# A decoder trunk with a mixture of experts on one Trainium2 core: the experts' down weights loaded as row pairs, the activation transposed by even and odd columns

## The reference

```python
D_MODEL = 1024; SEQ = 256; N_EXPERTS = 8; TOP_K = 2; D_FF_EXPERT = 3584
# moe_w_gate, moe_w_up: (1, 8, 1024, 3584)      moe_w_down: (1, 8, 3584, 1024)

def moe_swiglu(h, w_router, w_gate, w_up, w_down):
    t = h.reshape(-1, D)
    logits = (t @ w_router).astype(jnp.float32)
    top_v, top_i = lax.top_k(logits, TOP_K)
    top_w = jax.nn.softmax(top_v, axis=-1)
    combine = jnp.sum(jax.nn.one_hot(top_i, N_EXPERTS, dtype=jnp.float32) * top_w[..., None], axis=1)
    out = jnp.zeros_like(t)
    for e in range(N_EXPERTS):
        y = (jax.nn.silu(t @ w_gate[e]) * (t @ w_up[e])) @ w_down[e]
        out = out + combine[:, e:e + 1].astype(t.dtype) * y
    return out.reshape(B, S, D)
```

## Time and profile before

| | us |
|---|---|
| median of three runs | 1368.86 |
| the three runs | 1368.86, 1367.09, 1369.31 |
| the profiled execution, its own time | 1367.2 |
| its span (first to last instruction) | 1365.5 |
| PE busy | 1343.2 |
| DVE busy | 1086.4 |
| ACT busy | 924.5 |
| POOL busy | 127.3 |

### The profile page before, as it was taken

How to read it: one execution, slowest core, us unless ns; L and a number is a source line. 1 busy time by engine, 2 the same in 40 slices (tenths; PEclk the granted TensorE clock), 3 DMA queues, 4 the chain that set the end, 5 groups by cost and what they waited for, 6 DMA issues and landing times.

```text
span 1365.5 us, 17334 instructions
## 1 busy us (share of the span) xinstructions
PE 1343.2 (98%) x7271; PEld 1132.4 (83%) x7272; DVE 1086.4 (80%) x714; ACT 924.5 (68%) x755; POOL 127.3 (9%) x145
## 2 busy tenths in 40 slices
PE   8999999999999999999999999999999999999997
PEld 7878999989678888888888888888888888888885
DVE  5756444466768888888888888888888888888996
ACT  6664333355667777777777777777777777777774
POOL 3310000012124700000000000010000000000010
PEclk9999999999999999999999999999999999999999
DMA  9745555646439999999999999999999999999993
GB/s 317 230 148 183 185 185 185 201 129 214 143 124 285 395 391 369 397 389 377 388 391 364 371 395 383 368 397 389 369 376 396 374 377 383 394 370 376 397 396 145
DMA packets 200501, 431.78 MB, mean 316 GB/s; under 512 B 9697, under 2 KB 45793, under 8 KB 200418
## 3 DMA queue, kind: packets, MB, share of 16 engines
q1 hardware_dynamic: 195568, 416.19, 84.4%
q0 software_dynamic: 4848, 14.42, 2.9%
q10 hardware_dynamic: 2, 0.00, 0.0%
HBM read 418.58 MB, written 7.35 MB: 312 GB/s over the span
## 4 chain that ended last, share of the span: by engine, by line
PE 97%; DVE 1%; ACT 1%; issue 0%; DVEq 0%; ACTq 0%
PE ps L1243 94%; PE ps L1508 2%; PE ps L1270 0%; PE ps L1490 0%; DVE h_td L957 0%; PE ps L1377 0%; ACT work_a L783 0%; DVE xr L1144 0%; DVE w_low L932 0%; DVE hT_both L970 0%; ACT work_a L701 0%; ACT w_high L679 0%; ACT hT_both L717 0%; PE ps L1343 0%; DVE hpad L1010 0%
## 5 line engine op out<-in xcount | busy, mean ns | idle before, releaser
L932 DVE TENSOR_TENSOR w_low<-raw,w_high 128x2048 fp32r<-128x2048 f32 x390 | 899.6, 2308 | 201.6 <-ACT w_high L679 201.3
L679 ACT ACTIVATE w_high<-raw 128x2048 fp32r<-128x2048 f32 x390 | 747.1, 1916 | 265.0 <-PE ps L1243 265.0
L1243 PE MATMUL ps<-w_high,hT_both 128*128 128x512 f32 (+1 forms) x1920 | 599.6, 389 | 0.0
L1243 PEld LDWEIGHTS ps<-w_high,hT_both 128*128 128x128 f32 x1920 | 359.5, 188 | 71.5
L1243 PE MATMUL ps<-w_low,hT_both 128*128 128x512 f32 (+1 forms) x960 | 370.7, 386 | 0.0
L1243 PE MATMUL ps<-w_high,act_both 128*128 128x512 f32 x1072 | 342.0, 390 | 1.8 <-DVE act_both L1136 1.8
L1243 PEld LDWEIGHTS ps<-w_high,act_both 128*128 128x128 f32 x1072 | 201.3, 188 | 43.5 <-DVE act_both L1136 2.1
L1243 PEld LDWEIGHTS ps<-w_low,hT_both 128*128 128x128 f32 x960 | 181.0, 189 | 34.6
L1243 PE MATMUL ps<-w_low,act_both 128*128 128x512 f32 x536 | 208.7, 389 | 0.0
L1243 PE MATMUL ps<-hT_both,w_high 128*128 128x256 f32 x960 | 176.5, 284 | 1.1 <-DVE hT_both L970 1.1
L1243 PEld LDWEIGHTS ps<-hT_both,w_high 128*128 128x128 f32 x960 | 151.3, 192 | 2.3 <-issue 2.0
(11 more groups left out here) (254 smaller groups left out, 651.1 us busy)
## 6 DMA issues: line engine op xcount, KB each, us to landing
raw<-in_moe_w_gate SPq DMA_DIRECT2D x112, 1024.0 KB, 8.2
raw<-in_moe_w_up SPq DMA_DIRECT2D x112, 1024.0 KB, 7.9
raw<-in_moe_w_down SPq DMA_DIRECT2D x112, 1024.0 KB, 7.8
raw<-in_w_in SPq DMA_DIRECT2D x13, 1024.0 KB, 5.5
raw<-in_dense_w_gate SPq DMA_DIRECT2D x11, 1024.0 KB, 5.7
raw<-in_dense_w_up SPq DMA_DIRECT2D x11, 1024.0 KB, 5.5
raw<-in_dense_w_down SPq DMA_DIRECT2D x11, 1024.0 KB, 5.0
raw<-in_w_out SPq DMA_DIRECT2D x8, 1024.0 KB, 7.9
```

Source lines behind the costliest of these rows:

```text
L679: act.activation(w_part[0][:, s % PART_RING, :], raw[:, s % RAW_RING, :], ACT.Copy).then_inc(w_high_done, 1)
L932: dve.tensor_tensor(w_part[1][:, q, :], raw[:, r, :], w_part[0][:, q, :], ALU.subtract).then_inc(w_low_done, 1)
L1243: return pe.matmul(out_, lhsT, rhs, start=start, stop=stop, skip_group_check=True)
```

## The change

The view `ed_v` of the down weights now has pairs of neighbouring rows on a partition: row 256 c + 2 p + k. A load takes one value of c. On each partition the two rows are then 8 KB in one piece in HBM and 8 KB in one piece in SBUF. The bytes of a load, its slot, its issue and its wait are the same. Since piece k of a slot now holds the rows 2 p + k of its 256, the activation's piece f takes every second column: of the 256 columns of its half, the even ones for even f, the odd ones for odd f. The dense layer's down weights and all other weights keep their views.

```diff
@@ -321,7 +321,7 @@
-        ed_v = moe_w_down.rearrange("o e (k p) n -> (o e) p k n", p=P)
+        ed_v = moe_w_down.rearrange("o e (c p k) n -> (o e) c p k n", p=P, k=2)
@@ -430,7 +430,7 @@
             def down(s, e, g, i, per):
                 for j in range(2):
-                    load(s + j, ed_v[e, :, 4 * g + 2 * j:4 * g + 2 * j + 2, :], 2, i, per)
+                    load(s + j, ed_v[e, 2 * g + j, :, :, :], 2, i, per)
@@ -1505,7 +1505,7 @@
             def turn_act():
                 for f in range(4):
-                    last = pe.transpose(ps[:, 2, f * P:(f + 1) * P], prod_t[:, f * P:(f + 1) * P], ident[:, :])
+                    last = pe.transpose(ps[:, 2, f * P:(f + 1) * P], prod_t[:, f // 2 * 2 * P + f % 2:(f // 2 + 1) * 2 * P:2], ident[:, :])
                 last.then_inc(act_turned, 1)
```

## The result

| | before | after |
|---|---|---|
| median of 15 runs, us | 1368.16 | 1371.29 |
| lowest to highest, us | 1366.71 to 1370.13 | 1369.3 to 1372.95 |
| profiled execution / its span, us | 1367.2 / 1365.5 | 1370.79 / 1369.1 |

The ratio is 1.0021, with a 95% interval of 1.0014 to 1.0028: slower by 3.1 us. That is small, but clear of no change, and "no change" was forecast. The time lies inside the stated range; the direction was missed.

The account below looks back on a forecast made before the run. The prediction took PE to bound the kernel, with DMA close behind. Down loads 0 us and transposes 0 us left the profiled 1367.2 us unchanged, so a median of 1368.8 us, range 1365.5 to 1381 us.

Parts of the forecast that it names:

- the stated range: Range meant to hold in 8 of 10 cases for the kernel's median: 1365.5 to 1381 us.
- What bounds the kernel: Over the experts, 420 to 1346 us, PE sets the pace at 16.79 us a step, with DMA close behind.
- Part 1: Down loads in 8 KB pieces: about 0.38 us less DMA time a step, worth 0 us on the path.
- Part 2: Four transposes a step on line 1508, reading every second column: taken as 0 us, bounded by 0 and 31 us.
- The sum: Down loads 0 us plus transposes 0 us: profiled execution stays 1367.2 us, median 1368.8 us.
- my own middle bound: Strided transpose load on line 1508 takes 188 to 204 ns, 49 to 65 ns more: 8 to 15 us in all.
- The first rival: Strided load on line 1508 is slower and PE pays: 8 to 31 us, about 1380 us; chance 0.13.
- the rival's low price: Three of four transpose loads exposed at 49 ns more each, over 56 steps: 8 us.
- Transfers behind: Over the experts' steps, 8 KB pieces 20% slower make loads outlast PE: 16 us, about 1385 us; chance 0.07.
- a gain: Fewer packets make the 4032 matmuls of the 56 steps 1% closer: 9 us faster, about 1360 us; chance 0.07.
- pieces cut back: The queue cuts down-load pieces to 4 KB: packets stay 195,568, time as forecast; chance within the forecast's 0.73.
- the forecast's own range: Range of the kernel's median if nothing changes: 1366.5 to 1371 us; chance 0.73.

## Why the prediction was wrong, point by point

- **What bounds the kernel: right.** PE sets the pace before and after; no wait for a DMA in either.
- **Part 1, the down loads: right.** 181,232 packets, as said, and worth 0, as the run with only the row pairs shows. The relief was a little smaller than forecast: DMA share 1.01 instead of 1.00, median landing 7.5 us instead of 7.
- **Part 2, the four transposes: this is the step that failed.** The sum has them at 0 us because I took "the same instruction on contiguous data, 139 ns" for the strided one. Their term is 2.9 us. The load takes 201 ns, inside the 188 to 204 of my own middle bound. The 16-byte rule of the Trainium skill (SBUF — State Buffer, "Door 1: The DMA port swizzle") gave the same 0, and these runs disagree with it for a TensorE load: at 8 bytes apart each 16-byte line is hit twice and the load already costs its 62 ns more, while at 16 bytes apart it costs only 4 more. My argument that 150 ns for 128 columns left room rested on a misreading. In the trace before, the four loads start at 807.35, 807.58, 807.68 and about 807.79 us: the first runs ahead under the last matmul, the others are 0.10 to 0.11 us apart, and 150 ns is a mean with the first gap in it.
- **The first rival's mechanism was right, its size was not.** I wrote that "from the first extra nanosecond on it costs 3 to 4 times 56". Nor are three of four loads "exposed for sure": of 62 ns a load only about 12 are exposed a transpose, since successive loads overlap. What sets the transposes' pace, 108 ns and then 120, no run shows. In all it is 0.05 us a step, 2.9 us, where the rival's low price was 8. So both ends of my sum were off the truth that lay between them, 0 and 8, and the forecast took the wrong one of them.
- **Transfers behind; a gain; pieces cut back:** none came. More margin for the transfers moved nothing.
- **The chances.** 0.20 for slower was too low, with a load on the path for which the trace had no row at a stride and three nearby rows (188, 204 and 139 ns) that did not agree. The stated range reached to 1381 us for this rival alone; the forecast's own range ended at 1371, 0.3 us below what was measured.

## What to carry to other kernels

Before a layout is changed to please the DMA engines, ask who waits for a landing; here PE had no gap and nobody waited for a transfer, and the larger pieces were worth nothing. Then ask which engine reads the new layout: the stride belongs on the one with slack and a reading that does not care (here VectorE, 684 ns either way), not on TensorE's load. And when a record grows on an engine that overlaps its work, its price is what the chain shows of it, here a fifth, so bound the exposed share too, down to nothing.

## What the runs showed of the hardware that was not expected

- A 128-column fp32 transpose load takes 139 ns with adjacent elements, 201 at every second one (even or odd start), 205 at every fourth.
- Transposes in a row are paced at 108 ns each with contiguous loads, 120 with strided ones.
- A transpose between two 512-column matmuls is not cheaper than one among transposes, though its load is wholly covered: four apart cost 0.06 us a step more than four together where PE waits for nobody (16.85 us for 16.79).
